# One core of Trainium2: the samples' attention over caches and their matrix memory as two stages or as one unrolled stage of 16 steps

## The reference, cut to what matters

```python
# attention with forgetting, 16 heads of 64, over 512 cached keys and 16 new ones, per sample
k_all = concatenate([cache_k, k]); v_all = concatenate([cache_v, v])       # 528 positions
c_all = cumsum(concatenate([cache_logf, log_ff]))
s = q @ k_all.T * 64**-0.5 + cq[:, None] - ck[None, :]; s = where(causal, s, -inf)
y_f = softmax(s) @ v_all

# matrix memory, 4 heads of 256, one chunk of 16 tokens, per sample and head
D = tril(b[:, None] - b[None, :] + i);  g = b + m;  mt = maximum(g, max(D))
qk = (q @ k.T) * exp(D - mt)
num = exp(g - mt) * (q @ C) + qk @ v
h = num / maximum(|dot|, exp(-mt))
C_new = wC * C + (ws * k).T @ v                                             # 256x256 state
```

## Time and profile before

| | |
|---|---|
| median of 3 runs | 5664.45 us (5664.17 to 5665.58) |
| the profiled execution | 5658.33 us, of which the trace spans 5656.7 us |
| attention of the samples | first instruction at 827.03 us, last matmul ends at 1096.83 us |
| memory of the samples | first instruction at 1115.35 us, last DVE work ends at 1319.22 us |
| routing begins | 1324.25 us |
| PE busy over the span | 83%, with a mean granted clock of 0.879 |

### The profile page before, as it was taken

The page is one execution under the profiler, slowest core; times in us unless marked ns, Lnnn a source line. Parts: engine busy times, 40 slices in busy tenths (PEclk is TensorE's granted clock), DMA queues, the critical chain, the costliest instruction groups (busy, mean ns, idle before and its releaser), DMA issues. The chain is left out here.

```text
span 5656.7 us, 51607 instructions
## 1 busy us (share of the span) xinstructions
PE 4689.4 (83%) x16510; PEld 2846.4 (50%) x16510; DVE 3078.0 (54%) x6244; ACT 1030.8 (18%) x1850; POOL 1219.0 (22%) x1162
## 2 busy tenths in 40 slices
PE   4999678667984999957777758884699999999989
PEld 3555453343662555545555545564555545544544
DVE  1000231121476544468888861758877777777752
ACT  2000230001110111134444431111200000000013
POOL 0000002200002333223333320000044444444410
PEclk9999788767997999966666659997999999999999
DMA  3333323327755988778888868773599999999961
GB/s 100 108 114 105 99 83 128 108 86 270 276 197 197 356 306 311 284 272 322 331 323 320 317 243 326 275 255 119 190 381 419 418 412 419 411 419 418 414 263 58
DMA packets 464521, 1478.13 MB, mean 261 GB/s; under 512 B 38290, under 2 KB 204994, under 8 KB 361442
## 3 DMA queue, kind: packets, MB, share of 16 engines
q0 software_dynamic: 119872, 824.76, 36.5%
q1 hardware_dynamic: 344482, 651.36, 32.1%
HBM read 1370.06 MB, written 115.38 MB: 263 GB/s over the span
## 5 line engine op out<-in xcount | busy, mean ns | idle before, releaser
L1922 POOL DMA_INDIRECT ex_uv<-in_uv,ex_here x768 | 1049.2, 1366 | 1918.6 <-DVE ex_acc L1992 1783.6
L1979 DVE CUSTOM_DVE_ANT_0 ex_uv<-ex_uv,ex_xp 128x1024 f32<-128x1024 f32 x768 | 912.5, 1218 | 289.3 <-DMA ex_uv<-in_uv,ex_here 238.5
L1992 DVE SCALAR_TENSOR_TENSOR ex_acc<-ex_uv,ex_wt,ex_acc 128x1024 f32<-128x1024 f32 x768 | 941.8, 1282 | 9.5 <-DVE ex_wt L1983 1.1
L2261 PE MATMUL exp_psum_dn<-exp_dn_big,exp_dn_gg 128*128 128x512 f32 x1536 | 688.0, 598 | 28.4 <-DVE exp_dn_gg L2183 28.4
L2252 PE MATMUL exp_psum_dn<-exp_dn_xT,exp_dn_big 128*128 128x384 f32 x2048 | 683.5, 487 | 14.5 <-DMA exp_dn_big<-in_ud 14.5
L259 PE MATMUL proj_psum_acc<-proj_w,aT_later 128*128 128x385 f32 x1920 | 625.9, 488 | 74.2 <-DMA proj_w<-in_w_in 67.4
L2252 PEld LDWEIGHTS exp_psum_dn<-exp_dn_xT,exp_dn_big 128*128 128x128 f32 x2048 | 390.1, 191 | 314.2 <-issue 61.9
L259 PEld LDWEIGHTS proj_psum_acc<-proj_w,aT_later 128*128 128x128 f32 x1920 | 364.9, 190 | 334.8 <-issue 70.4
L259 PE MATMUL proj_psum_acc<-proj_w,aT 128*128 128x385 f32 x1536 | 499.7, 487 | 8.9 <-DMA proj_w<-in_w_in 8.9
L2261 PEld LDWEIGHTS exp_psum_dn<-exp_dn_big,exp_dn_gg 128*128 128x128 f32 x1536 | 292.4, 192 | 379.8 <-issue 352.3
L685 PE MATMUL att_psum_fy<-att_fv,att_fprobT 128*128 128x64 f32 x1152 | 238.4, 363 | 240.7 <-ACT att_fprobT L732 240.6
(11 more groups left out here) (368 smaller groups left out, 4864.2 us busy)
## 6 DMA issues: line engine op xcount, KB each, us to landing
proj_w<-in_w_in SPq DMA_DIRECT2D x48, 1540.0 KB, 7.1
rt_w<-in_w_q SPq DMA_DIRECT2D x36, 2048.0 KB, 8.3
exp_dn_big<-in_ud SPq DMA_DIRECT2D x128, 512.0 KB, 11.2
exp_dn_big<-in_vd SPq DMA_DIRECT2D x128, 512.0 KB, 8.0
scratch_z<-proj_zs SPq DMA_DIRECT2D x216, 192.5 KB, 2.7
rt_w<-in_w_br_m SPq DMA_DIRECT2D x18, 2048.0 KB, 10.8
rt_w<-in_w_br_f SPq DMA_DIRECT2D x18, 2048.0 KB, 10.9
rt_w<-in_w_out SPq DMA_DIRECT2D x18, 2048.0 KB, 8.2
```

What stands on the lines that cost most here:

```text
L1922: pool.indirect_dma_start(self.uv[:, slot * self.G + j, :], None, self.uv_tab, bass.IndirectOffsetOnAxis(ap=self.here[:, at, j:j + 1], axi ...
L1979: dve.tensor_tensor_reduce(self.uv[:, slot, 0:D], self.uv[:, slot, 0:D], self.xp[:], 1.0, 0.0, ALU.mult, ALU.add, self.dot[:, p % 2, j:j + ...
L1992: dve.scalar_tensor_tensor(out=self.acc[:, j % 2, :], in0=self.uv[:, slot, D:2 * D], scalar=self.wt[:, p % 2, j:j + 1], in1=self.acc[:, j ...
L2261: mm = pe.matmul(self.banks[t][:, n * 512:(n + 1) * 512], self.gg[:, 4 + q % 4, t * P:(t + 1) * P], self.big[:, 4 + q % 4, n * 512:(n + 1) ...
```

## The change

The two stages are replaced by one, `stage_sample`, without hardware loops. The attention becomes 16 steps (sample and group of heads), the memory 4 heads of 32 slots; each step carries 8 slots, in four quarters of two. Keys, values, `qd`, `kn` and the states `C` get two buffers each (the states' two buffers serve alternate heads). The attention's scores get one PSUM tile of two banks instead of two such tiles, and its turned probabilities and its outputs one bank each; the memory's eight banks become three that go round (`claim`, `full`, `free`). The mix of a step is put one step later, behind the scores of the next. q and k are turned through the one bank in four pieces, and ACT, not DVE, copies them out. The arithmetic is the same.

```diff
-            stage_fox_sample(nc, K, z, T)
-            stage_mlstm_sample(nc, K, z, gates, T)
+            stage_sample(nc, K, z, gates, T)
...
+class FoxSample:
...
+    def sp_k(self, sp, n):
+        if n >= 2:
+            sp.wait_ge(self.scored, 2 * n - 2)
+        sp.dma_start(self.kc[:, n % 2], ...).then_inc(self.kc_in[n % 2], 16)
+        sp.dma_start(self.ck[:, n % 2], ...).then_inc(self.kc_in[n % 2], 16)
+    def sp_v(self, sp, n):
+        if n == 1:
+            sp.wait_ge(self.t_full, 4)
+        if n >= 2:
+            sp.wait_ge(self.mixed, 2 * n - 2)
...
+    def sp_first(self, sp):
+        sp.dma_start(self.q, ...)
+        sp.dma_start(self.k, ...)
+        self.sp_k(sp, 0)
+        self.sp_v(sp, 0)
+        self.sp_k(sp, 1)
...
+    def pe_scores(self, pe, s):
+        if f == 0:
+            pe.wait_ge(self.placed, 5 * n + 5)
+            pe.wait_ge(self.kc_in[b], (n // 2 + 1) * 32)
+        if s >= 1:
+            pe.wait_ge(self.expd, s)
...
+    def pe_turn(self, pe, s, r):
+        pe.wait_ge(self.expd, s + 1)
+        pe.wait_ge(self.t_free, self.use(s, r))
...
+class MlstmSample:
+    SLOTS = 32
+    BANKS = 3
...
+    def claim(self, pe, n):
+        if n >= self.BANKS:
+            self.wait_free(pe, n - self.BANKS)
+        return self.bank[n % self.BANKS]
+    def sp_first(self, sp):
+        sp.dma_start(self.n_all ..., self.T["n0"])
+        for n in range(NSEQ):
+            sp.dma_start(self.m_all[...], self.T["m0"][n:n + 1, :] ...).then_inc(self.state_in, 16)
+        for i in range(2):
+            self.sp_state(sp, i)
+        self.sp_load(sp, 0)
+    def sp_step(self, sp, i, k):
+        if k == 14:
+            sp.wait_ge(self.y_head, i + 1)
+            sp.dma_start(self.T["ycat"][...], self.y[:])
+        if k == 28:
+            if i + 1 < H_M:
+                self.sp_load(sp, i + 1)
+            for n in range(NSEQ):
+                sp.wait_ge(self.c_set, i * 2 * NSEQ + 2 * n + 2)
+                sp.dma_start(self.T["mC_s"][n, i] ..., self.C[:, i % 2, n, :, 0:DM])
+            if i + 2 < H_M:
+                self.sp_state(sp, i + 2)
+    def pe_slot(self, pe, i, k):
+        if k == 1:    # sum of gates          (waits gates_in)
+        if k == 2:    # q, k turned           (waits z_in)
+        if k == 3:    # row exponents         (waits dx_set)
+        if k == 5:    # last, rows_m, s       (waits m_set, dm_set)
+        if k == 9:    # wp, n1, n2            (waits wp_set, mixed, placed, c_in)
+        if k >= 12 and k < 28 and k % 2 == 0:    # c0, c1 of one sample  (waits kw_set)
...
+    def dve_first(self, dve):
+        dve.memset(self.qd[:], 0.0).then_inc(self.set_up, 1)
+        dve.memset(self.v[:, DM:DM + 1], 1.0).then_inc(self.set_up, 1)
+        dve.wait_ge(self.set_up, 2)
+        dve.wait_ge(self.state_in, 16 * (NSEQ + 1))
...
+def stage_sample(nc, K, z, gates, T):
...
+        def _(sp):
+            fx.sp_first(sp)
+            ml.sp_first(sp)
+            for s in range(STEPS):
+                fx.sp_step(sp, s)            # s = 0: sp_v(1); f == 0: sp_k(n + 1); f == 1: sp_v(n + 1)
+                for quarter in range(4):
+                    for i, k in slots(s, quarter):
+                        ml.sp_step(sp, i, k)
+            ml.sp_last(sp)
...
+        def _(pe):
+            fx.pe_first(pe)
+            for s in range(STEPS + 1):
+                if s < STEPS:
+                    fx.pe_scores(pe, s)
+                for i, k in slots(s, 0):
+                    ml.pe_slot(pe, i, k)
+                if s >= 1:
+                    fx.pe_turn(pe, s - 1, 0)
+                for i, k in slots(s, 1):
+                    ml.pe_slot(pe, i, k)
+                if s >= 1:
+                    fx.pe_turn(pe, s - 1, 1)
+                for i, k in slots(s, 2):
+                    ml.pe_slot(pe, i, k)
+                if s >= 1:
+                    fx.pe_mix(pe, s - 1)
+                for i, k in slots(s, 3):
+                    ml.pe_slot(pe, i, k)
...
+        def _(dve):
+            ml.dve_first(dve)
+            fx.dve_first(dve)                # waits for q, k turned, then places sample 0
+            for s in range(STEPS + 1):
+                if s < STEPS:
+                    fx.dve_max(dve, s)
+                for quarter in range(3):
+                    for i, k in slots(s, quarter):
+                        ml.dve_slot(dve, i, k)
+                if s >= 1:
+                    fx.dve_y(dve, s - 1)     # waits mixed, then y
+                for i, k in slots(s, 3):
+                    ml.dve_slot(dve, i, k)
+                if s % 2 == 0 and s // 2 + 1 < NSEQ:
+                    fx.dve_place(dve, s // 2 + 1)
```

More of the change, by code:

```diff
@@ L1411, in diag8, with diag4, slots, _ @@
                    ap=[v.ap[0], [NSEQ * P, 2], [P + DSEQ, NSEQ], [1, DSEQ]])
+def diag4(flat, first):
+    step = P + 2 * DSEQ
+    v = flat[:, first:first + 3 * step + DSEQ]
+    return bass.AP(tensor=v.tensor, offset=v.offset, ap=[v.ap[0], [step, 4], [1, DSEQ]])
+def stage_sample(nc, K, z, gates, T):
+    with Stage(nc, "smp") as st:
+        fx = FoxSample(nc, K, st, z, T)
+        ml = MlstmSample(nc, K, st, z, gates, T)
+        STEPS = fx.STEPS
+        PER_STEP = H_M * ml.SLOTS // STEPS
+        QUARTER = PER_STEP // 4
+        def slots(s, quarter):
+            if s >= STEPS:
+                return []
+            at = s * PER_STEP + quarter * QUARTER
+            return [divmod(k, ml.SLOTS) for k in range(at, at + QUARTER)]
+        block = st.ctx.enter_context(nc.Block())
+        @block.sync
+        def _(sp):
[7 more added lines that the diff above has]
+            ml.sp_last(sp)
+        @block.gpsimd
+        def _(pool):
+            for s in range(STEPS):
+                fx.pool_y(pool, s)
+            fx.pool_last(pool)
+        @block.tensor
+        def _(pe):
[13 more added lines that the diff above has]
+                    ml.pe_slot(pe, i, k)
+                if s >= 1:
+                    fx.pe_mix(pe, s - 1)
+                for i, k in slots(s, 3):
+                    ml.pe_slot(pe, i, k)
+        @block.scalar
+        def _(act):
+            fx.act_first(act)
+            for s in range(STEPS + 1):
+                if s < STEPS:
+                    fx.act_exp(act, s)
+                for i, k in slots(s, 0):
+                    ml.act_slot(act, i, k)
+                if s >= 1:
+                    fx.act_probs(act, s - 1, 0)
+                for i, k in slots(s, 1):
+                    ml.act_slot(act, i, k)
+                if s >= 1:
+                    fx.act_probs(act, s - 1, 1)
+                for quarter in (2, 3):
+                    for i, k in slots(s, quarter):
+                        ml.act_slot(act, i, k)
+        @block.vector
+        def _(dve):
+            ml.dve_first(dve)
+            fx.dve_first(dve)
+            for s in range(STEPS + 1):
+                if s < STEPS:
+                    fx.dve_max(dve, s)
+                for quarter in range(3):
+                    for i, k in slots(s, quarter):
+                        ml.dve_slot(dve, i, k)
+                if s >= 1:
+                    fx.dve_y(dve, s - 1)
[3 more added lines that the diff above has]
+                    fx.dve_place(dve, s // 2 + 1)
```

762 lines of the change are left out of this document (416 added, 346 removed).

## The result

| | before | after |
|---|---|---|
| median | 5664.31 us (5662.77 to 5665.58) | 5519.88 us (5517.29 to 5521.03) |
| ratio, 95% interval | | 0.9743 (0.9728 to 0.9759) |
| span of the profiled execution | 5656.7 us | 5519.3 us |
| samples' stage(s), first instruction to routing's first load | 827.03 to 1324.25, 497.2 us | 830.20 to 1179.53, 349.3 us |

The change makes the kernel 144 us faster, where 81 were forecast. In the trace, the stage is 147.9 us shorter. It begins 3.2 us later than the two old stages did, and all behind it takes 7.3 us more (5519.3 - 1179.5 against 5656.7 - 1324.25). Both are within what the eleven traces of this document show for code that none of them changes: the stage begins between 826.8 and 833.1, and what follows it takes 4329.7 to 4339.8 us.

The account below looks back on a forecast made before the run. The old attention was taken as PE-bound, the memory as a chain of handoffs. Entry and step 0 to 873.2, plus 295.1, 7.0, 49 and 18.5, gave 1242.8, 81.4 us less: median 5583 us, range 5550 to 5635.

Parts of the forecast that it names:

- the end with POOL's drain: Last mix to the next stage's first instruction: 18.5 us kept from the old attention, including 10.5 us in which POOL drains.
- PE's work: PE's matrix work in the merged stage at full clock: 70.5 us per four steps with a head, not lowered by the change.
- the lower clock: Merged stage behind step 0: 163 us if all ran at the lower clock, times a share of 0.30, 49 us.
- the waits: PE's waits left by the new order in the merged stage: 8.1 us a head, making 78.6 us for four steps.
- The banks: PE's waits for a free PSUM bank in the memory's slots: 0.2 us in a head's second step, 1.7 in third and fourth.
- the wait of some 5 us for q and k in step 0: Slot 2 of step 0 waits for head 0's q and k, loaded behind both heads' states: scores end 860.8, data about 866.
- The entry: Stage start: small vectors land behind a second keys load at 850, so scores start at 851.5 against 839.16 before.
- Rival 1: More is covered in the merged stage: half the waits vanish, 0.15 of time at the lower clock; 5542 us, chance 0.08.
- Rival 2: The lists do not interleave: 50 us of memory idle return, lower-clock share 0.45 adds 24; 5657 us, chance 0.07.
- Rival 3: A load on SP's list is late every second step, 5 us each, 40 us less gain; 5623 us, chance 0.06.
- rival 4: PE's clock stays down in the merged stage: gain falls to 6 us, or 5697 us at worst; chance 0.05.
- The rule on banks that cycle: Skill page's rule: PE cycling through PSUM banks with short idles swings its clock; at its worst it is rival 4.

Follow-up runs that it names:

- experiment 5: The changed kernel with PE also waiting, behind each step's scores, for that step's exponential: 0.9807 of the kernel before, 5548.9 us.
- experiments 2: The changed kernel not interleaved, all 16 attention steps and then all 128 memory slots: 0.9867 of the kernel before, 5587.3 us.
- experiment 3: The kernel before with a second pair of banks for the c products of odd samples, nothing else changed: 0.9906, 5610.9 us.
- experiment 1: The changed kernel with one buffer each for keys, values and states instead of two: 0.9744 of the kernel before, stage 345.3 us.
- experiment 4: The changed kernel with four banks going round for the memory instead of three: 0.9746 of the kernel before, stage 348.7 us.
- experiment 8: The changed kernel with SP instead of POOL issuing the stores of y; alone, 0.9719 of the kernel before, 5507.5 us.

## Why the prediction was right and wrong

Right: the direction, that PE's list is what the stage lasts, that no load or store holds its body up, that the second buffers are not what brings the time, and the end with POOL's drain (17.7 us against 18.5). The total was 63 us too high, beyond the range; I had given 0.08 to the rival on that side. What failed is the price of all three terms of the body: PE's work, the lower clock and the waits were each sized too high by 22 to 26 us, two thirds of it in the terms for waits and clock. Of what the changed profile was to show, the clock (0.90), PE's share of 94%, steps of 15.4 (fourth) and 26.6 us (second) and the drain of 10.5 us came as said; a head took 74.7 us instead of 85 to 95, and the routing's first load came at 1179.5 instead of 1243. The terms of the body:

| term, first scores to last mix | forecast | measured | difference |
|---|---|---|---|
| PE's work at the full clock | 4 x 70.5 = 282 | about 4 x 65 = 260 (an estimate, see below) | -22 |
| lower clock | 49 + 3 = 52 | 286.3 - 260 = 26 | -26 |
| waits | the rest, 39 | 303.6 - 286.3 = 17.3 | -22 |
| sum | 372.8 | 303.6 | -69 |

The body's 69 less, a first score 3.5 us later counted from the stage's start (28.0 against 24.5) and an end of 0.8 less make the stage's 66.5 (81.4 forecast, 147.9 found).

**PE's work.** Here the step that failed is, for about half of the 22 us, adding durations. A row's duration holds a tail that the next row overlaps; only start to start adds up. Behind one another in the changed stage, at the full clock:

```profile
972.93 1.14 PE L1379 MATMUL smp_psum_n<-smp_nv,smp_nkw 128*128 128x257 f32 x4
973.90 3.60 PE L1123 MATMUL smp_psum_ss<-smp_skc,smp_sqd 128*128 128x512 f32 x8
...
980.04 1.11 PE L1379 MATMUL smp_psum_n<-smp_nv,smp_nkw 128*128 128x257 f32 x4
980.99 0.60 PE L1135 MATMUL smp_psum_st<-ident,smp_sprob 128*128 128x128 f32 x4
981.43 1.10 PE L1379 MATMUL smp_psum_n<-smp_nv,smp_nkw 128*128 128x257 f32 x4
982.38 0.27 PE L1137 MATMUL smp_psum_st<-ident,smp_sprob 128*16 128x128 f32 x1
982.54 1.33 PE L1379 MATMUL smp_psum_n<-smp_nv,smp_nkw 128*128 128x257 f32 x4
983.70 3.60 PE L1149 MATMUL smp_psum_sy<-smp_svc,smp_sprobT 128*128 128x512 f32 x8
987.23 1.12 PE L1151 MATMUL smp_psum_sy<-smp_svn,smp_sprobT 16*128 16x512 f32 x2
988.28 1.14 PE L1379 MATMUL smp_psum_n<-smp_nv,smp_nkw 128*128 128x257 f32 x4
989.25 3.60 PE L1123 MATMUL smp_psum_ss<-smp_skc,smp_sqd 128*128 128x512 f32 x8
```

A c sample costs 0.97 (973.90 - 972.93), not 1.13; scores 6.14; the turn 0.60; the mix 988.28 - 983.70 = 4.58, not 4.76. The state product is 8.3 us in its quickest head of four (about 8.1 from start to start), where the earlier trace rows had one at mixed clocks. The small products leave about 4 us a head at the full clock (an estimate: most of their pairs lie 0.25 to 0.3 us apart there), not 5.6. A head: 4 x 11.3 + 8 x 0.97 + 8.1 + 4 = 65. Of the 5.5 us a head between this and 70.5, turns, mixes and c products make 2.4 (durations added), the state product 1.0, the small products 1.6 (my guess of 5.6 had no row at the full clock under it) and the scores 0.4. The step from 973.90 to 989.25 takes 15.35 us with not one wait in it. The Trainium skill, page "Perfetto Trace Analysis", section "Tensor Engine Instruction (MATMUL, LD_WEIGHTS)", says that the end of such an instruction is computed, not observed; the overlapping rows agree (973.90 lies inside the row that starts at 972.93 and lasts 1.14).

**The lower clock.** The share of 0.30 was read off stages with more idle time (the prompt's has PE busy 79%, this one 94%). It came out at 2 x (1 - 0.90) = 0.20, which by my own price of 163 us would be 33. The rest of the miss is where the lower clock falls: hardly on the long blocks, whose instructions take 592 ns at the full clock and 628 (scores) and 605 (mixes) in the mean, against 786 and 731 before, but on those of 257 columns, which take 380 at the full clock and 459 and 451 in the mean. I put the two terms side by side as if they were free of each other; experiment 5, where a wait alone was added and the clock fell with it, shows that they are not, and experiments 2 and 3 agree.

**The waits.** Of my 8.1 us a head, 4.2 were found. The chains that I listed exist for the most part, but they are shorter: 1.07, 0.65, 1.03, 0.77 and 0.34 us in the second head, 3.9 in all, where the prediction had 1.9, 0.8 + 0.4, 1.3 + 0.6, 0.9 and 0.3, or 6.2. The banks cost nothing (1.9 a head in the sum), and the wait of some 5 us for q and k in step 0 did not come: they are turned at 867.82, with no transfer as releaser.

**The entry.** The transfers ahead of the vectors were sized nearly right (the vectors 23 us after the start by my sum, 25 in the trace), but not that DVE clears `sqd` only behind its wait for them:

```profile
855.23 1.76 DVE L1155 MEMSET smp_sqd<- 128x2048 f32 x1 [22.75 <-DMA smp_nm_all<-in_m]
```

The vectors landed at 855.2, with 24 us of transfers at a share of 0.97 ahead of them, and clearing, placing and handoff add 3 us.

**The cause was seen too narrowly.** The text puts the whole gain down to attention covering the memory's chains. Taken one after another, the parts of the 147.9 us are these. 54 can be had from the banks going round, which the diff shows as `claim` and which I read only as a possible wait; that is shown on the kernel before itself. About 22 more come with the single stage without interleaving. They are 43 us gained, less a start that costs 16 us more and an attention 5 us longer. Of the 43, some 24 are the stretch ahead of the memory's first product (25.3 us, now 1.1), in which the barrier with POOL's drain and the wait for the memory's own vectors lie; what brings the other 19 was not tried. The other 72 are the interleaving. This order of counting is a choice: the prediction counted the c products' waits among those that attention covers, and whether interleaving would have covered them with the old pair of banks was not tried. So the banks do not explain the miss; the table's terms do.

**The rivals.** Rival 1 (5542) was on the right side, and its share of the lower clock (0.15, found 0.20) and its waits (half, found 17 of 39 us) are close; it still had PE's work 22 us too high. Rival 2 wanted more than 60 us of idle time in the body, and 17 were found. Rival 3 is out since no transfer is among PE's releasers, even in experiment 1, and rival 4 by the clock of 0.90. The rule on banks that cycle: experiment 3 has more cycling and a clock of 0.76 instead of 0.62, experiment 4 changes nothing. In the kernel before, banks that go round took idle time away, and the clock rose with it. The Trainium skill, page "TensorE: Matmul & The Clock Gate", section "A second HAM failure mode: psum-queue depth-cycling", describes the swing for cycling that leaves short idle times between groups; no run here shows cycling as such to do harm.

## What to carry to other kernels

Before two stages are interleaved, look at the banks of the one that idles: if PE fills a pair and waits until it is read, a second pair costs four lines and gave 54 us here, before anything was interleaved. Price PE's work from start to start, never by adding durations, and price idle time on PE with the clock that it costs, not as a term of its own. At the entry and exit of a stage, see what stands ahead of the few small vectors that the first instruction needs, and whether the last act is a store that POOL issues. These two were worth 14 and 7 to 10 us here.

## What the runs showed of the hardware

- **Idle time on PE is paid nearly twice.** Interleaving took away 46 us of idle time and 38 of busy time (0.84 for each); the banks in the kernel before 31 and 24 (0.78); the added wait gave 17.4 and 13.4 (0.77). It is no fixed ratio: without the step-late mix 2 us of idle time came with 8 of busy time. Where the idle time falls may matter; these runs do not say.
- **POOL's drain is there because POOL issues transfers.** It took 10.5 us in both kernels, and was gone where SP issued the same 128 stores, each at about 0.44 us of SP's time (in experiment 8, alone, eight from 1142.77 took 3.54 us). In a stage where POOL computed and issued no transfer the drain took 0.04 us.
- **34 KB late cost up to 14 us.** With the transfers' share at 0.97, nine small vectors asked for behind some 7 MB of q, k and caches landed 25 us after the stage's first instruction; asked for ahead of the first values, and with DVE's clearing moved ahead of the wait for them, they held nothing up.
